# Gate, up and down projections: high weights times high and low values in one matmul of 512 columns, halves summed on VectorE

## What is computed

```python
# layer 1
h = rms_norm(x, g_ffn_pre[l]) * (1.0 + scale_f[:, None]) + shift_f[:, None]
ff = (jax.nn.silu(h @ w_gate[l]) * (h @ w_up[l])) @ w_down[l]
x = x + gate_f[:, None] * rms_norm(ff, g_ffn_post[l])
```

## Time and profile before

| | before |
|---|---|
| median of 3 runs | 2812.94 us (2812.19 to 2818.18) |
| the profiled execution, its own time | 2820.23 us |
| its span, first to last instruction | 2818.4 us |
| mean granted clock of TensorE | 0.945 |
| matmuls, and weight loads | 19936 each |
| moved by DMA | 503.83 MB |

### The profile page before, as it was taken

How to read it: one execution, slowest core, us unless ns; L and a number is a source line. 1 busy time by engine, 2 the same in 40 slices (tenths; PEclk the granted TensorE clock), 3 DMA queues, 4 the chain that set the end, 5 groups by cost and what they waited for, 6 DMA issues and landing times. The chain is left out here.

```text
span 2818.4 us, 47985 instructions
## 1 busy us (share of the span) xinstructions
PE 2606.4 (92%) x19936; PEld 2404.8 (85%) x19936; DVE 1433.0 (51%) x1866; ACT 1040.0 (37%) x1322; POOL 284.3 (10%) x369
## 2 busy tenths in 40 slices
PE   5999988969999999999789979799899999999998
PEld 3888846949999999999779937358799999999998
DVE  3577756856764444344353354524455555554443
ACT  3523244334333343333243325223344444443332
POOL 4000121420000000011221000101100000000000
PEclk8999989979999999999889979779899999999999
DMA  8777866936775555555535402003455555554553
GB/s 300 260 278 271 258 215 236 330 110 237 259 272 184 181 191 179 170 188 181 156 106 170 151 15 75 15 1 120 141 172 180 181 186 181 179 179 165 179 190 108
DMA packets 263852, 503.83 MB, mean 179 GB/s; under 512 B 17168, under 2 KB 26299, under 8 KB 263483
## 3 DMA queue, kind: packets, MB, share of 16 engines
q1 hardware_dynamic: 249888, 492.99, 52.2%
q10 hardware_dynamic: 13867, 9.50, 1.3%
HBM read 498.05 MB, written 2.10 MB: 177 GB/s over the span
## 5 line engine op out<-in xcount | busy, mean ns | idle before, releaser
L1220 DVE TENSOR_TENSOR w_lo<-raw,w_hi 128x2048 fp32r<-128x2048 f32 (+2 forms) x386 | 862.1, 2233 | 1019.9 <-ACT w_hi L776 1019.3
L1788 PE MATMUL bank<-x_hi,w_hi 128*128 128x256 f32 (+3 forms) x4608 | 1314.1, 285 | 51.6 <-DVE w_lo L1220 18.8
L1789 PE MATMUL bank<-x_lo,w_hi 128*128 128x256 f32 (+3 forms) x4608 | 1311.0, 284 | 0.0
L1790 PE MATMUL bank<-x_hi,w_lo 128*128 128x256 f32 (+3 forms) x4608 | 1309.0, 284 | 0.0
L776 ACT ACTIVATE w_hi<-raw 128x2048 fp32r<-128x2048 f32 (+2 forms) x386 | 719.4, 1864 | 1070.2 <-PE bank L1790 919.1
L1788 PEld LDWEIGHTS bank<-x_hi,w_hi 128*128 128x128 f32 (+1 forms) x4608 | 876.9, 190 | 77.7 <-DVE w_lo L1220 38.6
L1790 PEld LDWEIGHTS bank<-x_hi,w_lo 128*128 128x128 f32 (+1 forms) x4608 | 877.9, 191 | 0.0
L1789 PEld LDWEIGHTS bank<-x_lo,w_hi 128*128 128x128 f32 (+1 forms) x4608 | 873.7, 190 | 0.2 <-issue 0.2
L1788 PE MATMUL bank<-hid_hi,w_hi 128*128 128x256 f32 x1408 | 400.6, 285 | 7.9 <-POOL hid_lo L662 6.6
L1789 PE MATMUL bank<-hid_lo,w_hi 128*128 128x256 f32 x1408 | 399.9, 284 | 0.0
L1790 PE MATMUL bank<-hid_hi,w_lo 128*128 128x256 f32 x1408 | 399.8, 284 | 0.0
(11 more groups left out here) (279 smaller groups left out, 1545.3 us busy)
## 6 DMA issues: line engine op xcount, KB each, us to landing
raw<-in_w_ada SPq DMA_DIRECT2D x88, 1024.0 KB, 6.0
raw<-in_w_gate SPq DMA_DIRECT2D x88, 1024.0 KB, 5.2
raw<-in_w_up SPq DMA_DIRECT2D x88, 1024.0 KB, 5.2
raw<-in_w_in SPq DMA_DIRECT2D x68, 1024.0 KB, 5.7
raw<-in_w_down SPq DMA_DIRECT2D x64, 1024.0 KB, 5.0
raw<-in_w_down SPq DMA_DIRECT2D x32, 768.0 KB, 4.3
raw<-in_w_o SPq DMA_DIRECT2D x16, 1024.0 KB, 6.9
raw<-in_w_out SPq DMA_DIRECT2D x16, 1024.0 KB, 5.1
```

The lines of the kernel that those rows point to most:

```text
L1220: dve.tensor_tensor(w_lo[ps][:, 0:width], raw[slot][:, 0:width], w_hi[ps][:, 0:width], ALU.subtract).then_inc(raw_free[slot], 1)
L1788: pe.matmul(out, wh[:, k, c], hi(k0 + k), start=a0, stop=False)
L1789: pe.matmul(out, wh[:, k, c], lo(k0 + k), start=False, stop=False)
L1790: ins = pe.matmul(out, wl_[:, k, c], hi(k0 + k), start=False, stop=z)
```

## The change

For gate and up of layer 1, up of layer 2 and down of both, `dense` gets `both`: one matmul with w_hi streams x_hi and x_lo of one k as 512 columns into both halves of a bank, and one with w_lo streams x_hi into the first half. The pairs lie in one tensor (x_both, hid_both), at the same addresses as before. Who empties a bank now adds the halves. Layer 1 gate: VectorE reduces each bank to gpad behind the `rest` of the up half's first unit (q == 3), and ScalarE's Silu works in place on gpad, behind its next split. Up: `up_by_gate` reduces to sq and multiplies from there. Layer 1 down: VectorE reduces to branch_f in place of ScalarE's copy. Layer 2 down: a second add onto x_res, chained ahead of the first. On ScalarE the making of hid_hi moves behind the first split of the next block (`hidden_high`), and in layer 2 the split of the up half's second unit moves ahead of the fourth gate tile. Layer 2 gate, all in- and out-projections, and the loads stay as they are.

```diff
-        x_hi = place("x_hi", [P, KT, N2], F32R)
...
-        x_lo = place("x_lo", [P, KT, N2], F32R)
+        x_both = place("x_both", [P, 2, KT, N2], F32R)
+        x_lo_at = x_hi_at + 4 * KT * N2
+        x_hi, x_lo = x_both[:, 0, :, :], x_both[:, 1, :, :]
...
-        hid_hi = place("hid_hi", [P, FT, S], F32R)
-        hid_lo = place("hid_lo", [P, FT, S], F32R)
+        hid_both = place("hid_both", [P, 2, FT, S], F32R)
+        hid_hi, hid_lo = hid_both[:, 0, :, :], hid_both[:, 1, :, :]
...
# ScalarE
+            def hidden_high(i, before=0):
+
                 for m in range(4):
-                    act.wait_ge(up_freed, 4 + i * 4 + m + 1)
+                    act.wait_ge(up_freed, 4 + (i + before) * 4 + m + 1)
                     act.activation(hid_hi[:, bass.ds(i * 4 + m, 1), :].rearrange("p a n -> p (a n)"),
                                    gpad[:, m, 0:S], ACT.Copy).then_inc(hid_high, 1)
+
+            def mlp1(i, before=None, with_ada=False, first=False):
+                step = 1 if with_ada else 0
+                for j in range(1, 5):
+                    if before:
+                        before(j)
+                    split(skip=step, used=j - 1, tiles=0 if j == 1 else None)
+                    if j == 1 and not first:
+                        hidden_high(i - 1)
+                su.at += 3
                 t.at += 4
+                for j in range(1, 5):
+                    split(used=j - 1, tiles=0 if j == 1 else None)
+                    if j == 1:
+                        if with_ada:
+                            take_ada(bank[7][:, 0:4])
+                        for m in range(4):
+                            act.wait_ge(bank_freed, 4 + 4 * BLOCKS_OUT1 + i * 4 + m + 1)
+                            act.activation(gpad[:, m, 0:S], gpad[:, m, 0:S], ACT.Silu).then_inc(gate_silu, 1)
+                su.at += 3
+                t.at += 4
...
             def down1(i):
                 split_block(12)
-                for m in range(4):
-                    take(m, lambda b: act.activation(branch_f[:, bass.ds(i * 4 + m, 1), :].rearrange(
-                        "p a n -> p (a n)"), b[:, 0:S], ACT.Copy))
                 t.at += 4
...
-            def mlp2(i, before=None):
-                split_block(4, before=before)
+            def mlp2(i, before=None, first=False):
+                for j in range(1, 5):
+                    if before:
+                        before(j)
+                    split(used=j - 1, tiles=0 if j == 1 else None)
+                    if j == 1 and not first:
+                        hidden_high(i - 1, 11)
+                su.at += 3
                 for m in range(4):
+                    if m == 3:
+                        split(tiles=4)
                     act.wait_ge(hid_low, (i + 11) * 4 + m + 1)
...
# VectorE
+            def halves(b):
+
+                return bank[b][:, :].rearrange("p (t n) -> p n t", t=2)
+
+            def up_by_gate(m):
+
+                u_ = sq[:, m % 2, 0:S]
+                chain(dve.tensor_reduce(u_, halves(4 + m), AX, ALU.add))
+                dve.tensor_tensor(gpad[:, m, 0:S], u_, gpad[:, m, 0:S], ALU.mult).then_inc(up_freed, 1)
+
...
                     rest()
+                    if q == 3:
+                        for m in range(4):
+                            dve.wait_ge(hid_low, i * 4 + m + 1)
+                            dve.wait_ge(tile_done, (BLOCKS_OUT1 + 1) * 4 + i * 8 + m + 1)
+                            dve.tensor_reduce(gpad[:, m, 0:S], halves(m), AX, ALU.add).then_inc(bank_freed, 1)
                 for m in range(4):
-
+                    dve.wait_ge(gate_silu, i * 4 + m + 1)
                     dve.wait_ge(tile_done, (BLOCKS_OUT1 + 2) * 4 + i * 8 + m + 1)
-                    dve.tensor_tensor(gpad[:, m, 0:S], bank[4 + m][:, 0:S], gpad[:, m, 0:S], ALU.mult).then_inc(
-                        up_freed, 1)
+                    up_by_gate(m)
...
             def down1(i):
                 for j in range(1, 13):
                     rest(3 * COLS if 8 <= j < 12 else UK * COLS)
+                for m in range(4):
+                    dve.wait_ge(tile_done, 4 + 4 * (BLOCKS_OUT1 + 22) + i * 4 + m + 1)
+                    dve.tensor_reduce(branch_f[:, bass.ds(i * 4 + m, 1), :].rearrange("p a n -> p (a n)"), halves(m),
+                                      AX, ALU.add).then_inc(bank_freed, 1)
...
+                if both:
+                    chain(dve.tensor_tensor(t_, t_, bank[m][:, b:2 * b], ALU.add))
                 dve.tensor_tensor(t_, t_, bank[m][:, 0:b], ALU.add).then_inc(bank_freed, 1)
...
# TensorE
+                            if both is not None:
+                                pair_out = bank[base + m][0:r, 0:2 * n].rearrange("p (t n) -> p t n", t=2)
+                                if z:
+                                    pe.matmul(out, wl_[:, k, c], hi(k0 + k), start=False, stop=False)
+                                    ins = pe.matmul(pair_out, wh[:, k, c], both(k0 + k), start=False, stop=True)
+                                else:
+                                    pe.matmul(pair_out, wh[:, k, c], both(k0 + k), start=a0, stop=False)
+                                    ins = pe.matmul(out, wl_[:, k, c], hi(k0 + k), start=False, stop=False)
+                                continue
```

More of the change, by code:

```diff
@@ L1057, in _ @@
             squares("ffn_pre", lambda j: act.wait_ge(added, j + 1))
-            def mlp1(i, before=None, with_ada=False):
-                split_block(4, skip=1 if with_ada else 0, before=before)
+            def hidden_high(i, before=0):
                 for m in range(4):
[L1062 to L1067, removed]
-                for m in range(4):
-                    act.wait_ge(up_freed, 4 + i * 4 + m + 1)
+                    act.wait_ge(up_freed, 4 + (i + before) * 4 + m + 1)
                     act.activation(hid_hi[:, bass.ds(i * 4 + m, 1), :].rearrange("p a n -> p (a n)"),
                                    gpad[:, m, 0:S], ACT.Copy).then_inc(hid_high, 1)
-                t.at += 4
-            mlp1(0, quarters("ffn_pre"))
+            def mlp1(i, before=None, with_ada=False, first=False):
[7 more added lines that the diff above has]
+                su.at += 3
+                t.at += 4
+                for j in range(1, 5):
[8 more added lines that the diff above has]
+                t.at += 4
+            mlp1(0, quarters("ffn_pre"), first=True)
             loop(4, (8, 8, 1, 12, 4), lambda i: mlp1(i + 1, with_ada=True))
             loop(6, (8, 8, 0, 8, 4), lambda i: mlp1(i + 5))
+            hidden_high(10)
             act.wait_ge(tile_done, 4 + 4 * (BLOCKS_OUT1 + 22))
@@ L1175, in mlp2 @@
                 t.at += 4
-                for m in range(5):
+                for m in range(1, 5):
                     if m < 4:
[L1178 to L1181, removed]
+                        split(used=m)
+                    act.wait_ge(conv_ready, i * 4 + m)
+                    act.activation(gpad[:, m - 1, 0:S], tmp[:, (m - 1) % 2, 0:S], ACT.Silu).then_inc(silu_ready, 1)
                 su.at += 3
[L1183 to L1186, removed]
                 t.at += 4
-            mlp2(0, quarters("ffn2"))
+            mlp2(0, quarters("ffn2"), first=True)
             loop(10, (8, 8, 0, 8, 4), lambda i: mlp2(i + 1))
+            hidden_high(10, 11)
             def down2(i):
@@ L1692, in _, with onto_residual @@
             statistics("mla_out")
-            def onto_residual(i, m, first, b):
+            def onto_residual(i, m, first, b, both=False):
                 dve.wait_ge(tile_done, 4 + first + i * 4 + m + 1)
@@ L1749, in _ @@
             for m in range(4):
-                onto_residual(3, m, 4 * (BLOCKS_OUT2 + 22), S)
+                onto_residual(3, m, 4 * (BLOCKS_OUT2 + 22), S, both=True)
         @block.tensor
@@ L2126, in mlp1 @@
             def mlp1(i, ready=None, ada_block=None):
-                dense(K16, FOUR, *xs(S), S, ready=ready, step=1 if ada_block is None else 2)
+                dense(K16, FOUR, *xs(S), S, ready=ready, step=1 if ada_block is None else 2, both=xb)
                 if ada_block is not None:
@@ L2130, in mlp1 @@
                     ada_sum(ada_block, bank[7])
-                dense(K16, FOUR, *xs(S), S, base=4, bank7=None if ada_block is None else ada_block + 1)
+                dense(K16, FOUR, *xs(S), S, base=4, bank7=None if ada_block is None else ada_block + 1,
+                      both=xb)
             mlp1(0, quarters("ffn_pre"))
@@ L2137, in down @@
             def down(i, **more):
-                dense(K44, FOUR, lambda k: hid_hi[:, k, :], lambda k: hid_lo[:, k, :], S, **more)
+                dense(K44, FOUR, lambda k: hid_hi[:, k, :], lambda k: hid_lo[:, k, :], S,
+                      both=lambda k: hid_both[:, :, k, :], **more)
             loop(4, (12, 4, 12), down)
@@ L2226, in mlp2 @@
                 dense(K16, FOUR, *xs(NC), NC, ready=ready)
-                dense(K16, FOUR, *xs(S), S, base=4)
```

(1 more changed line is left out.)

20 lines of the change are left out of this document (10 added, 10 removed).

## The result

| | before | after |
|---|---|---|
| median, same chip (8 runs each) | 2816.39 us | 2845.70 us |
| lowest to highest | 2812.06 to 2832.08 | 2842.26 to 2851.75 |
| profiled execution | 2820.23 us (span 2818.4) | 2842.47 us (span 2840.7) |
| TensorE: matmuls, busy | 19936, 2606.4 us | 16416, 2589.5 us |
| VectorE busy | 1433.0 us | 1554.4 us |

The ratio is 1.0099, 95% interval 1.0080 to 1.0117: the change costs 29 us (the medians) where 11 us of gain were forecast. 2845.7 lies above the range's 2838, on the other side of no change.

What follows compares the result with a forecast made beforehand. TensorE's array time was taken to bound the gate, up and down stages. A matmul gain of 43 us less losses of 16, 4, 7 and 4.6 gave -11 us, 2802 us off the median of 2812.9; range 2771 to 2838.

Steps and rivals of the forecast that it cites:

- The bound: Gate, up and down stages with hardly a gap: TensorE's array time bounds them, so a change pays by array time alone.
- The price of 512 columns: Each 512-column matmul in 3520 triples: fixed extra of 12 ns per instruction, 225 ns, gain 43 us; chance 0.42.
- The reduction: VectorE's sum over pairs in PSUM: 0.69 us each, 1.07 us per tile with the multiply, 4.3 for four.
- Slow reduce: Rival: the reduce takes 1.3 us, 2.5 us more at each of 22 block ends, 2857 us; chance 0.10.
- (a): Four ada blocks of layer 1: TensorE's stand grows from 1.0 to 3.8 us with half clock behind, 16 us lost.
- (b): Plain blocks of layer 1, no ada work between: w_lo still in time, cost nothing, with 0.1 us of cover.
- (c): Layer 2 gate/up: pairs hold VectorE, TensorE's stand grows from 0.4 to 0.8 us in ten blocks, 4 us lost.
- (d): Before each down, TensorE's wait for the last hid_lo grows by 2.6 us, plus longer half clock: 7 us lost.
- (e): Down block boundaries: layer 1 waits for VectorE's reduce, layer 2 for two adds instead of one; 4.6 us lost.
- proportional columns: Rival at each 512-column matmul: cost grows with columns, 236 ns, 5 us gained in all, 2835 us; chance 0.30.
- It does nothing: Rival: the program loads and streams weights as before, only the losses stay, 2845 us; chance 0.02.
- Nearly free: Rival: the 12 ns vanish under 512 columns, 216 ns each, a further 32 us gained, 2773 us; chance 0.16.

Runs made afterwards that it cites:

- matmul-only kernel: Kernel before with the 512-column matmul in all 3520 triples, second bank halves never added up: 0.9916, 2797.82 us against 2817.63.
- experiment 2: matmul-only kernel with down's operands as one run of 512 (layer 1) or two of 192 (layer 2); only spacing read: 384 columns 175 ns, 512 236.

## Why the prediction was wrong

- **The bound** (array time in these stages): right. The matmul-only kernel gains what its spacing says, 22.5 us for 3520 triples, 6.4 ns each.
- **The price of 512 columns** (225 ns, "the 12 ns belong to the instruction"): wrong, and the first step that failed. It is 231 with x and 230 to 236 with hidden, so the term is -22.5 and not -43 (at 236 the hidden triple saves 7 ns and not 4, because the 256 columns beside it fall from 119.9 to 117.3). The evidence was in the rows: 272 columns took 7.8 ns more than 256, of which I called 6.7 plain columns and dismissed the 1.1 as smaller than the difference between operands. Per column that is 0.49 ns, and experiment 2 found 0.46. The argument from half clock (the extra vanishes, so it is fixed) did not follow: it only shows that the extra belongs to full clock, not that it belongs to the instruction. I also set the point of decision at 228 ns, and 231 to 236 lie beyond it. The rule of the Trainium skill that I weighed (TensorE: Matmul & The Clock Gate, "Wait — 56ns, not 53.3ns?", a fixed 2.5 ns) would have erred more: by it the matmuls would have gained 75 us.
- **The reduction** (0.69 us, pair 1.07, four 4.3): right, 0.684 measured. *Slow reduce* falls.
- **(a) Ada blocks** (3.8 us and half clock, 16 us): right in mechanism, 3.9 us at a clock of 0.64; against the matmul-only kernel these four blocks lose 17.0. But the size was met by luck: 6 us of it went with the clash, which the forecast did not have. The longer queue alone makes a stand of 2.6 us and costs 10.9 (8.8 and 2.1) of the 16, with the clock at full speed behind two of the four stands.
- **(b) Plain blocks** ("cost nothing, with 0.1 us of cover"): wrong. They stand 0.6 us, 3.2 us for the five in the stretch of 108 to 144 and 4.1 for all six. I had written that all would wait if the cover went, which they do, and did not ask what a moved step on ScalarE does to GpSimd, and GpSimd to VectorE. I said "POOL's lows are needed three units later", which is true and beside the point: what counted was what ran beside them.
- **(c) Layer 2** (4 us): wrong by its largest amount. 17.7 us against the matmul-only kernel: a stand of 1.8 us instead of 0.8 in ten blocks, and half clock behind three of them. With the clash removed it is the 0.85 us forecast.
- **(d), (e) The waits before down and the boundaries** (7 and 4.6 us): right within their size. The waits grew by 1.9 and 2.1 us where 2.6 each was forecast (the first, 4.5 us, lies under the 5 to 6.5 that I gave); a boundary of down stands 1.1 us in layer 1 and 1.3 in layer 2 between starts, 0.4 and 0.6 before. Against the matmul-only kernel the stretches with the waits lose 3.9 and 3.7 us, the rest of the two downs 3.2 and 2.1: 12.9 against 11.6 for both terms.
- **The sum.** -43 + 32 = -11 became -22.5 + 51 = +28.8. Half of the miss is the price of the columns (20 us), half are waits (19 us), and there the clash, which no rival had, is alone worth 25. Without it the waits come to 26 us, 6 less than forecast, nearly all of that in (a). Of the rivals *proportional columns* (2835 us) came nearest in its cause: it had the sign and the first half of what happened, though with 5 us of gain left it went too far on the columns. *It does nothing* (2845 us) has the measured number by chance: the program has 3520 matmuls less and the matmul-only kernel gained 24 us. *Nearly free* and *slow reduce* fall by the spacing and by 0.684 us.

## What to carry to other kernels

Read an unknown price from the slope between the two shapes that the trace does have before you call its excess fixed; 7.8 ns over 16 columns was the better witness than a shape at half rate. Where an edit moves a step off one engine, look up what it releases on a third, what then runs beside it, and which of the two begins first: here one condition (behind the first split or the second) was worth 26 of the 29 us that the change cost. And try a change stage by stage: the same matmul pays in down and in the blocks with room on VectorE, and loses where VectorE's queue is what the next unit waits for.

## What the runs showed of the hardware

- At a granted clock of 1.00 a matmul of this type costs 0.46 ns per column start to start (117, 175 and 230 to 236 ns for 256, 384 and 512 columns), 10% over the bare columns at 2.4 GHz; at 1.2 GHz the bare columns. One run of 512 and two of 256 cost the same.
- Of a VectorE operation with both inputs in SBUF and a GpSimd subtraction that meet, the one that began second took the delay: VectorE's multiply 0.43 to 0.99 us and split 2.29 to 2.83 behind a running subtraction, a subtraction 0.7 to 2.4 behind a running split, whose 2.29 us stayed. VectorE's reductions from PSUM (0.68) and its multiplies with one operand in PSUM (0.41 to 0.43) kept their time either way.
- Stands of 2.04 to 2.11 us between starts, in ten like blocks, were followed three times by half clock and seven times not; ten of 1.96 to 2.01 never, four of 4.2 always.
